# Halving the planes of squares once more in two of five norms of a two-layer decoder trunk

## The reference

```
hn = rms_norm(h, norm_mix_pre[i])
m  = mixer_i(hn)                      # layer 0: delta rule heads + stick-breaking attention; layer 1: S5 scan, gelu, gated unit
h  = h + rms_norm(m, norm_mix_post[i])
hn = rms_norm(h, norm_ffn_pre[i])
f  = (silu(hn @ w_gate) * (hn @ w_up)) @ w_down
h  = h + rms_norm(f, norm_ffn_post[i])
```

## Time and profile before

| | us |
|---|---|
| median of 3 runs | 2748.02 |
| lowest and highest | 2747.98, 2749.83 |
| span of the profiled execution | 2748.7 |
| TensorE busy | 2678.9 |
| VectorE busy | 1266.2 |
| GpSimd busy | 1015.0 |
| ScalarE busy | 626.3 |

### The profile page before, as it was taken

How to read it: one execution, slowest core, us unless ns; L and a number is a source line. 1 busy time by engine, 2 the same in 40 slices (tenths; PEclk the granted TensorE clock), 3 DMA queues, 4 the chain that set the end, 5 groups by cost and what they waited for, 6 DMA issues and landing times.

```text
span 2748.7 us, 44704 instructions
## 1 busy us (share of the span) xinstructions
PE 2678.9 (97%) x18073; PEld 2555.5 (93%) x18073; DVE 1266.2 (46%) x2119; ACT 626.3 (23%) x1108; POOL 1015.0 (37%) x462
## 2 busy tenths in 40 slices
PE   8999999999999999999999999899999999999998
PEld 7999788866999999999999989899899999999997
DVE  5666667566174444444442457612632222222235
ACT  4231333365151000000000342411420000000002
POOL 5444110034354444444333325052544444444440
PEclk9999999999999999999999999999999999999999
DMA  4236321110232222222223139641231111111112
GB/s 163 93 109 136 97 69 57 49 62 25 87 113 67 76 82 82 82 78 79 81 76 96 52 124 283 219 115 42 98 108 46 46 46 46 46 46 46 46 31 82
DMA packets 142550, 232.27 MB, mean 84 GB/s; under 512 B 34016, under 2 KB 104928, under 8 KB 140256
## 3 DMA queue, kind: packets, MB, share of 16 engines
q1 hardware_dynamic: 53552, 134.98, 15.9%
q10 hardware_dynamic: 88880, 95.59, 11.0%
HBM read 172.78 MB, written 61.96 MB: 85 GB/s over the span
## 4 chain that ended last, share of the span: by engine, by line
PE 89%; DVE 6%; ACT 2%; issue 2%; DMA 1%; POOL 0%; ACTq 0%; DVEq 0%; POOLq 0%
PE psum L806 25%; PE psum L807 24%; PE psum L808 24%; PE psum L892 2%; PE psum L1295 2%; PE psum L1269 1%; DVE area L2282 1%; DVE area L2249 1%; PE psum L1117 1%; DVE x_lo L2294 1%; PE psum L1282 1%; PE psum L1138 1%; PE psum L1387 1%; DMA resid<-area 1%; DVE area L2272 1%
## 5 line engine op out<-in xcount | busy, mean ns | idle before, releaser
L806 PE MATMUL psum<-x_hi,w_hi 128*128 128x344 f32 (+2 forms) x3456 | 1123.9, 325 | 0.7 <-issue 0.7
L807 PE MATMUL psum<-x_lo,w_hi 128*128 128x344 f32 (+2 forms) x3456 | 1105.5, 320 | 0.0
L808 PE MATMUL psum<-x_hi,w_lo 128*128 128x344 f32 (+2 forms) x3456 | 1104.9, 320 | 0.0
L764 POOL TENSOR_TENSOR w_hi<-stage,const 128x1024 fp32r<-128x1024 f32 x193 | 484.6, 2511 | 1515.0 <-PE psum L808 1346.5
L806 PEld LDWEIGHTS psum<-x_hi,w_hi 128*128 128x128 f32 x3456 | 650.0, 188 | 11.1 <-issue 3.7
L807 PEld LDWEIGHTS psum<-x_lo,w_hi 128*128 128x128 f32 x3456 | 650.0, 188 | 3.3 <-issue 1.7
L808 PEld LDWEIGHTS psum<-x_hi,w_lo 128*128 128x128 f32 x3456 | 649.4, 188 | 0.0
L767 POOL TENSOR_TENSOR w_lo<-stage,w_hi 128x1024 fp32r<-128x1024 f32 x193 | 486.3, 2520 | 15.1
L2754 DVE TENSOR_TENSOR area<-area,psum 128x344 f32<-128x344 f32 (+2 forms) x132 | 67.7, 513 | 653.4 <-ACT area L1971 653.4
L806 PE MATMUL psum<-act_hi,w_hi 128*128 128x344 f32 (+2 forms) x1056 | 341.6, 323 | 8.3 <-DVE area L2777 6.9
L808 PE MATMUL psum<-act_hi,w_lo 128*128 128x344 f32 (+2 forms) x1056 | 336.9, 319 | 0.0
(11 more groups left out here) (235 smaller groups left out, 2233.8 us busy)
## 6 DMA issues: line engine op xcount, KB each, us to landing
stage<-wstream SPq DMA_DIRECT2D x193, 512.0 KB, 3.5
s_set<-area ACTq DMA_DIRECT2D x8, 1600.0 KB, 7.1
proj<-area ACTq DMA_DIRECT2D x20, 520.0 KB, 2.7
area<-proj ACTq DMA_DIRECT2D x36, 256.0 KB, 3.7
resid<-area ACTq DMA_DIRECT2D x6, 1376.0 KB, 6.0
area<-resid ACTq DMA_DIRECT2D x6, 1376.0 KB, 11.4
area<-s SPq DMA_DIRECT2D x8, 1024.0 KB, 6.7
area<-proj ACTq DMA_DIRECT2D x12, 520.0 KB, 4.8
```

Source lines behind the costliest of these rows:

```text
L764: pool.tensor_tensor(per_block(w_hi[:, slot, :]), src, ones_block, ALU.mult).then_inc(high_split, 1)
L806: mm(out[:, 0:n], w_hi[:, slot, wk], hi[:, xk, a:a + n], start=first, stop=False)
L807: mm(out[:, 0:n], w_hi[:, slot, wk], lo[:, xk, a:a + n], start=False, stop=False)
L808: return mm(out[:, 0:n], w_lo[:, slot, wk], hi[:, xk, a:a + n], start=False, stop=last)
```

## The change

For thirds 0 and 1 of r = 1 and r = 3 VectorE folds twice: the 8 planes to 4 as before, and then the upper 2 of these 4 onto the lower 2. TensorE multiplies 2 planes instead of 4 there. Between the two additions VectorE waits for its own counter. Third 2 of both places, and the other norms, stay as they were. Eight sums are concerned: two thirds, two sums each, two places.

```diff
+        def folded_twice(r, c):
+            return folded(r) and c < 2
...
-                planes = KT // 2 if folded(r) else KT
+                planes = KT // 4 if folded_twice(r, c) else KT // 2 if folded(r) else KT
...
                 low, high = (x[:, :, 0:n] for x in sq_halves)
-                V.tensor_tensor(low, low, high, add).then_inc(nm_folded, 1)
+                if not folded_twice(r, c):
+                    V.tensor_tensor(low, low, high, add).then_inc(nm_folded, 1)
+                    return
+                ch(V.tensor_tensor(low, low, high, add))
+                ch.sync()
+                V.tensor_tensor(low[:, 0:2], low[:, 0:2], low[:, 2:4], add).then_inc(nm_folded, 1)
```

## The result

The changed kernel takes 2753.3 us (median of 13 runs, 2749.11 to 2755.79), the kernel before 2748.48 us over 13 runs on the same chip. The ratio is 1.0015 with a 95% interval of 1.0008 to 1.0022: slower by 4.1 us, 2.2 to 6.0, and by 4.8 between the medians. The forecast was a time of 2754.0 and a difference of +5.9. The time is met more closely than the difference, in part because the median before, of 13 runs now, is 0.5 higher than the one that the forecast was put on.

What follows compares the result with a forecast made beforehand. TensorE, busy 97%, was taken as the bound, with VectorE already late at some sums. +1.66 + 2.3 + 2.66 - 0.7 = +5.9 us, put on the median of 2748.02, gave 2754 us; forecast's own range 2752 to 2757, overall 2746 to 2758.

Steps and rivals of the forecast that it cites:

- Third 0: Both layers, GpSimd idle: second addition of 0.92 hidden in slack; TensorE 2.36 us ahead in the first layer, 2.26 second.
- Sum (1,0): First layer, third 1: second addition waits for a GpSimd instruction; TensorE idles 3.3 us, then is 0.58 ahead.
- Sum (1,1), first layer: VectorE's chain without slack, turns with GpSimd: sum starts 3.53 us later, TensorE 2.37 late behind it.
- Sum (2,0): First layer, third 2: fold ends before the later TensorE arrives, so the former wait of 0.71 us is gone.
- The clock in the first layer: After a wait of 5.0 us at (1,1) TensorE's clock falls: +2.3 us, bounds 0 and 3.1.
- the list: The prediction's step-by-step start and end times of VectorE, GpSimd and TensorE; first layer +1.66 us at full clock.
- The second layer: Same steps as the first layer: +2.66 us, less 0.7 for a low clock already there before.
- a further loss: Rival: one more turn lost or 3.3 us waits at (1,0) lower the clock: +2 to +3 more; chance 0.08.
- its next instruction starts at 1950.58 and goes first: Second layer: GpSimd precedes the residual addition, ready at 1950.75, by 0.17 us; otherwise the layer's sum is +0.57.
- Straight behind: Rival: second addition follows the first without GpSimd between, costing 0.76; -4.6 us, 2743.4; chance 0.11.
- Planes alone: Rival: folds find GpSimd not yet started, none is held, whole 9.26 us gained: 2738.8; chance 0.06.

Runs made afterwards that it cites:

- third 0 alone: Changed kernel with the double fold kept only for third 0, in both layers; 2745.55 us, ratio 0.9985 against the kernel before.
- the kernel that keeps it up: Changed kernel plus 6 and 10 unread constant products in TensorE ahead of sums (1,0) and (1,1); 2749.94 us, ratio 1.0002 against the kernel before.
- the second layer alone: Changed kernel with the double fold of both thirds only in the second layer (r = 3); 2750.54 us, ratio 1.0002 against the kernel before.
- two holds and third 0 alone: Double fold in third 0 only; GpSimd's first feed-forward slab waits for fold (1,0), its third for fold (1,1); 2742.61 us, ratio 0.9980 against before.
- two holds and both thirds: Changed kernel; GpSimd's first feed-forward slab waits for fold (1,0), its third for fold (1,1); 2746.53 us, ratio 0.9993 against the kernel before.
- the first layer alone: Changed kernel with the double fold of both thirds only in the first layer (r = 1); 2752.32 us, ratio 1.0015 against the kernel before.
- the kernel with the reduction: Changed kernel with third 1's second addition made a tensor_reduce with one SBUF operand of twice the size; 2743.62 us, ratio 0.9985 against before.

## Why the prediction was right

*Third 0.* Hidden in both layers, 0.89 long, and worth its 2.36 and 2.26: third 0 alone shortened the stretches by 2.36 and 2.24. The root that VectorE waits for came 1.78 us earlier in the first layer, where 1.76 was predicted and TensorE gained 2.36, and it did follow the table load without a gap. Right.

*Sum (1,0).* Predicted a wait of 3.3; measured 3.32 in both layers. The second addition from GpSimd's end to its own end 0.74, predicted 0.73. Right.

*Sum (1,1), first layer.* Predicted a start 21.53 us behind (1,0) and a wait of 5.0; measured 21.50 and 4.97. Right, and with it the assumption that line 2294 and the residual additions keep their places in the order of turns.

*Sum (2,0).* Predicted without a wait; so it was.

*The clock in the first layer.* Taken as +2.3, measured as 2.17 by the kernel that keeps it up. It was the middle of two losses read at other places, 3.1 and 1.45, and not worked out for this one; so the fall was forecast, but the close agreement of its size is luck. Without it the stretch is 80.21, +1.39 on before, where the list had +1.66.

*The second layer.* Predicted +2.66 - 0.7 = +2.0, measured +0.75. Two things were off. The wait at (1,0) let the clock fall as well, which I had among the rivals as a further loss. And the sentence that failed is "its next instruction starts at 1950.58 and goes first". Counted from the start of the sum (0,0), the list had GpSimd's fourth slab start at 40.30 us and the residual addition ready at 40.47. The addition was ready at 40.44, and GpSimd did go first, but with an earlier instruction: it had stood idle for 2.50 us until TensorE, slowed by its clock, had freed the slot of the third slab (in the first layer, with the same wait and no fall, it did not stand idle). What ran ahead of the addition was the second instruction of that third slab, begun at 39.01 and so 1.3 us sooner. The addition took 2.41 instead of the 3.68 of the list, and the wait at (1,1) became 5.61 rather than over 8.

The kernel with the second layer alone bears this out. Its TensorE, GpSimd and VectorE, and the clock behind (1,0):

```profile
1962.59 2.63 PE L896 MATMUL psum<-area,const 128*128 128x344 f32 x4 [8.27 <-DVE area L2281]
...
1943.14 2.72 POOL L768 TENSOR_TENSOR w_hi<-stage,const 128x1024 fp32r<-128x1024 f32 x1 [0.96 <-PE psum L812]
...
1948.58 3.57 DVE L2263 TENSOR_TENSOR area<-area 128x1376 f32<-128x1376 f32 x1
...
1935.00:1940.00 5.00, 3.55 (x11) 2.63 (x12) 5.00 (x3) 0.00 (x0) 4.92 (x3) 0.66 0.35 108
1940.00:1945.00 5.00, 5.00 (x33) 5.00 (x33) 4.02 (x2) 0.80 (x1) 4.04 (x2) 1.00 0.30 98
```

Here the low clock lasted 3.4 us (0.66 over 5) instead of 6.9 (0.67 and 0.64 over 5 each). GpSimd stood idle for 0.96 only, the residual addition took 3.57, and the wait at (1,1) was 8.27, as the list had it. The stretch is +1.41 against +0.75 in the changed kernel. So the longer fall did not cost more: a loss of TensorE's clock was paid back by GpSimd's idleness.

*Rivals.* Straight behind: refuted by 2.90, with a GpSimd instruction ended 0.74 before the end. Planes alone: refuted by the same rows, GpSimd had started at 765.56 and the first addition at 767.23. The margins were as in the list.

The sum of the steps was +5.9, the medians give +4.8, of which the two stretches show +4.3. The size that was off is the second layer's, by 1.2; the first layer's is off by 0.4 (3.56 against 3.96).

## What to carry to other kernels

When two engines take turns by whole instructions, an added instruction can cost its own length and one of the other engine's, however short it is (0.9 became 2.9 here); so split the edit by where the other engine is idle (here four of the eight folds gained 4 us and the other four lost 8). If the work must be done beside GpSimd, a form with one SBUF operand was cheaper even at twice the elements (1.60 against 2.90; alone the addition takes 0.88). A neighbour's work that is pushed away comes due elsewhere: look at who waits for it, and from when.

## What the runs showed that I had not expected

A waiting GpSimd does not always go before VectorE's next instruction. In the kernel with two holds and third 0 alone, GpSimd's instruction was issued at 767.26, behind the first of line 2294 (2305 here) at 767.01, and both instructions of that line ran (3.16 together, unstretched) before it:

```profile
767.01 3.16 DVE L2305 TENSOR_TENSOR x_lo<-area,x_hi 128x1408 fp32r<-128x1408 f32 x2
...
767.26 5.17 POOL L770 TENSOR_TENSOR w_hi<-stage,const 128x1024 fp32r<-128x1024 f32 x1 [50.59 <-DVE area L2279]
```

The same happened in its second layer (5.02 us at 1930.33). In the kernel with two holds and both thirds GpSimd, issued 0.26 us behind the first of the pair, went between them (3.63). What decides it is open.

Two waits of 3.32 us before the same sum had different ends: the clock stayed at 2.4 GHz in the first layer and fell in the second. It is no matter of the layer: with the first layer alone, the same code with a wait of 3.31 let it fall in the first. Nor does the length of the wait alone decide: in the kernel with the reduction it fell at (1,0) of the second layer with a wait of 2.03 (granted 0.67 from 1935 to 1940), and the sum of 2 planes lasted 2.18 instead of 1.4. What decides it is open, so a wait of 2 to 5 us cannot be given a price of the clock in advance from these runs, only a range.
